# Second attention of a two-block kernel: scores of 64 rows in split precision, the bias added by the vector engine

## The reference

```python
q = rms_norm_2((h @ w_q).reshape(bsz, seqlen, N_HEADS, 2, HEAD_DIM), q_norm)
# k, v from shared_kv: k normed the same way, v has 128 columns a head
rel = k_pos[None, :] - q_pos[:, None]
bias = rel_bias[t5_causal_bucket(rel)].transpose(2, 0, 1)
s = jnp.einsum("bqhcd,bkhcd->bhcqk", qc, k) * HEAD_DIM ** -0.5
s = jnp.where(rel <= 0, s + bias[None, :, None], NEG_INF_2)
pm = jax.nn.softmax(s, axis=-1)
attn = pm[:, :, 0] - lam * pm[:, :, 1]
out = jnp.einsum("bhqk,bkhe->bqhe", attn, v)
```

## Time and profile before

| | |
|---|---|
| median of 3 runs | 2324.82 us |
| the profiled execution | 2324.46 us |
| its span | 2322.7 us |
| PE busy | 2128.9 us (92%) |
| DVE busy | 1281.0 us (55%) |
| ACT busy | 819.9 us (35%) |
| POOL busy | 466.5 us (20%) |
| mean granted clock of PE | 0.955 |

### The profile page before, as it was taken

How to read it: one execution, slowest core, us unless ns; L and a number is a source line. 1 busy time by engine, 2 the same in 40 slices (tenths; PEclk the granted TensorE clock), 3 DMA queues, 4 the chain that set the end, 5 groups by cost and what they waited for, 6 DMA issues and landing times.

```text
span 2322.7 us, 27094 instructions
## 1 busy us (share of the span) xinstructions
PE 2128.9 (92%) x9788; PEld 1681.1 (72%) x9788; DVE 1281.0 (55%) x1733; ACT 819.9 (35%) x1309; POOL 466.5 (20%) x596
## 2 busy tenths in 40 slices
PE   8999999999999454799999999999977899999999
PEld 8987668888887354687787877665655577877877
DVE  4253356464355698347747466633366467556455
ACT  3123333122235345534424234432144344334233
POOL 4052017970015784010000001100131000000000
PEclk9999989999999777899999999999899899999999
DMA  4220022232322100122222323221100122323222
GB/s 141 90 73 1 1 73 91 91 100 90 100 91 74 35 1 1 65 91 82 91 99 90 109 82 104 89 69 63 59 19 10 46 82 91 109 80 106 79 98 100
DMA packets 48592, 172.16 MB, mean 74 GB/s; under 512 B 5806, under 2 KB 6318, under 8 KB 48492
## 3 DMA queue, kind: packets, MB, share of 16 engines
q1 hardware_dynamic: 47164, 166.46, 21.6%
q0 software_dynamic: 1328, 4.37, 0.6%
HBM read 168.68 MB, written 2.12 MB: 74 GB/s over the span
## 4 chain that ended last, share of the span: by engine, by line
PE 84%; DVE 8%; ACT 5%; issue 2%; POOL 0%; DMA 0%; DVEq 0%; SPq 0%; ACTq 0%; POOLq 0%
PE ps L393 65%; PE ps L555 6%; PE ps L517 2%; ACT sq L1061 2%; PE ps L1390 1%; PE ps L499 1%; DVE t L1075 1%; PE ps L690 1%; ACT u_t L839 1%; PE ps L691 1%; PE ps L711 1%; PE ps L1392 1%; PE ps L1410 1%; ACT t L1458 1%; PE ps L1026 1%
## 5 line engine op out<-in xcount | busy, mean ns | idle before, releaser
L393 PE MATMUL ps<-x_hi,w_hi 128*128 128x512 f32 x1280 | 513.2, 401 | 5.0 <-DVE w_lo L379 4.9
L393 PE MATMUL ps<-x_lo,w_hi 128*128 128x512 f32 x1280 | 507.1, 396 | 0.0
L393 PE MATMUL ps<-x_hi,w_lo 128*128 128x512 f32 x1280 | 506.4, 396 | 0.0
L379 DVE TENSOR_TENSOR w_lo<-raw,w_hi 128x1024 fp32r<-128x1024 f32 x308 | 395.6, 1287 | 165.1 <-ACT w_hi L375 165.1
L375 ACT ACTIVATE w_hi<-raw 128x1024 fp32r<-128x1024 f32 x308 | 321.8, 1049 | 308.0 <-PE ps L393 136.6
L393 PE MATMUL ps<-a_hi,w_hi 128*128 128x512 f32 x928 | 372.0, 401 | 19.1 <-DVEq L360 11.2
L393 PE MATMUL ps<-a_hi,w_lo 128*128 128x512 f32 x928 | 369.6, 398 | 0.0
L393 PE MATMUL ps<-a_lo,w_hi 128*128 128x512 f32 x928 | 369.5, 398 | 0.0
L393 PEld LDWEIGHTS ps<-x_hi,w_hi 128*128 128x128 f32 x1280 | 241.1, 188 | 86.4 <-issue 22.2
L445 POOL TENSOR_TENSOR t<-t,sq 128x512 f32<-128x512 f32 x49 | 71.4, 1456 | 1116.0 <-ACT sq L436 1115.0
L393 PEld LDWEIGHTS ps<-x_lo,w_hi 128*128 128x128 f32 x1280 | 241.3, 189 | 56.8 <-issue 1.7
(11 more groups left out here) (322 smaller groups left out, 2704.7 us busy)
## 6 DMA issues: line engine op xcount, KB each, us to landing
raw<-in_wstream SPq DMA_DIRECT2D x308, 512.0 KB, 3.3
h<-in_xT SPq DMA_DIRECT2D x4, 528.0 KB, 7.3
b_raw<-scratch POOLq DMA_DIRECT2D x8, 256.0 KB, 3.5
out<-h SPq DMA_DIRECT2D x8, 256.0 KB, 2.0
p_raw<-in_pT POOLq DMA_DIRECT2D x2, 512.0 KB, 4.6
b_in_<-in_ssm_bc POOLq DMA_DIRECT2D x1, 512.0 KB, 4.3
c_raw<-in_ssm_bc POOLq DMA_DIRECT2D x1, 512.0 KB, 6.2
vecs<-in_vecs SPq DMA_DIRECT2D x1, 294.0 KB, 3.8
```

The costliest lines, as they stand in the source:

```text
L379: e.tensor_tensor(w_lo[:, u.slot, :], raw[:, u.c % 2, :], w_hi[:, u.slot, :], ALU.subtract)\
L393: last = e.matmul(ps[:, bank, :], wt[:, u.slot, w], x[:, k0 + k, 0:SEQ], start=(k == 0 and n == 0), stop=(k == kt - 1 and n == 2))
```

## The change

- The scores of a map are three fp32r products over that map's 64 rows (`q_hi` by `k_hi`, `q_hi` by `k_lo`, `q_lo` by `k_hi`). The scale is in q's norm gain (`gain_q`). `q_hi`, `k_hi` are written by ACT and `q_lo`, `k_lo` by POOL during the k and v projections; `k_hi` lies over `q2`, `k_lo` over `k2`. POOL's staging tiles go, `v` is turned from `v2` itself.
- The bias is added by DVE: `tensor_tensor_reduce` reads the scores from PSUM and the bias tile from SBUF, writes minus the sum into one of three SBUF tiles (`t0`, `t1`, `t2`) and gives the minimum. It takes the place of the maximum. The exponentials read from that tile in place. `b_hi`, `b_lo` and the flipped identity go.
- For this the bias rows must come in order: POOL writes each table row 128 times to DRAM, with a pitch of 641, and reads it back with a pitch of 640 (`bias_rows`, `bias_load`). Two bias tiles take turns.
- The order: PE does the scores of g, transposes of g-2, value products of g-3; DVE the maxima of g, then the mix of g-1; ACT copies the turned v after the exponentials; only the value products wait for it. The mix takes one reciprocal for both maps.
- The score slots are free when DVE's pass is done.

```diff
     with ExitStack() as c:
-        qs2 = sb("qs2", [P, 2, 2, SEQ], F32, c)
-        ks2 = sb("ks2", [P, 2, SEQ], F32, c)
-        vs2 = sb("vs2", [P, 2, SEQ], F32, c)
-        vtok = sb("vtok", [P, 2, 4, P], F32, c)
-        pt2 = sb("pt2", [P, 2, 4, P], F32, c)
-        b_hi = sb("b_hi", [P, 2, SEQ], F32R, c)
-        b_lo = sb("b_lo", [P, 2, SEQ], F32R, c)
+        q_hi = sb("q_hi", [P, 8, SEQ], F32R, c)
+        q_lo = sb("q_lo", [P, 8, SEQ], F32R, c)
     sb("region_a", [P, 2 * KT * SEQ])
...
+    with ExitStack() as c:
+        vtok = sb("vtok", [P, 2, 4, P], F32, c)
+        pt2 = sb("pt2", [P, 2, 4, P], F32, c)
+        bias1 = sb("bias1", [P, SEQ], F32, c)
     sb("region_x", [P, 2 * KT * TOK])
...
     with ExitStack() as c:
+        k_hi = sb("k_hi", [P, 8, SEQ], F32R, c)
+        k_lo = sb("k_lo", [P, 8, SEQ], F32R, c)
+    with ExitStack() as c:
         q2 = sb("q2", [P, 8, SEQ], F32, c)
...
-    scratch = nc.dram_tensor("scratch", (8, 640), F32, kind="Internal").ap()
+    scratch = nc.dram_tensor("scratch", (8, P * 641), F32, kind="Internal").ap()
...
+                if who == "act" and b > 1:
+                    qk_act(e, b, m - 1)
                 last(m - 1)
...
+    def qk_act(e, b, m):
+        e.wait_ge(hn_y, 8 * (b - 1) + m + 1)
+        if b == 3:
+            e.wait_ge(qk_lo, m + 1)
+        to, of = (q_hi, q2) if b == 2 else (k_hi, k2)
+        e.activation(to[:, m, :], of[:, m, :], ACT.Copy).then_inc(qk_hi, 1)
+
+    def qk_pool(e, b, m):
+        e.wait_ge(qk_hi, 8 * (b - 2) + m + 1)
+        e.wait_ge(hn_y, 8 * (b - 1) + m + 1)
+        hi, lo, of = (q_hi, q_lo, q2) if b == 2 else (k_hi, k_lo, k2)
+        e.tensor_tensor(lo[:, m, :], of[:, m, :], hi[:, m, :], ALU.subtract).then_inc(qk_lo, 1)
...
     def bias_load(e, p):
         if p >= 2:
-            e.wait_ge(s_mm, 32 + 4 * (p - 1))
...
+            e.wait_ge(nb_ok, 32 + 8 * (p - 1))
+        src = bass.AP(scratch.tensor, scratch.offset + p * P * 641 + P, [[640, P], [1, SEQ]])
+        e.dma_start((bias0, bias1)[p % 2][:, :], src).then_inc(b_in[p % 2], 16)
+
+    def bias_rows(e, p):
+        dst = bass.AP(scratch.tensor, scratch.offset + p * P * 641, [[P * 641, 1], [641, P], [1, 640]])
+        e.dma_start(dst, tab[p:p + 1, :].unsqueeze(1).to_broadcast([1, P, 640])).then_inc(tab_out, 16)
+
+    ST = (t0, t1, t2)
...
+        def pe_values(p):
+            ge(e, o_ok, p - 1)
+            for j in range(4):
+                last = e.transpose(ps[:, 6 + p % 2, j * P:(j + 1) * P], v2[:, p, j * P:(j + 1) * P], ident[:, :])
+            last.then_inc(vt_mm, 1)
+
         def pe_scores(g):
...
-            ge(e, exp_ok, 32 + 2 * (g - 1))
-            for c in range(2):
-                o = ps[:, 2 * sl + c, 0:N]
-                e.matmul(o, qs2[:, p % 2, c, qt * P:(qt + 1) * P], ks2[:, p % 2, 0:N], start=True, stop=False)
-                for n, t in enumerate((b_hi, b_lo)):
-                    last = e.matmul(o, flip_r[:, :], t[:, p % 2, SEQ - N:SEQ], start=False, stop=(n == 1))
+            if g >= 2:
+                e.wait_ge(nb_ok, 32 + 2 * (g - 1))
+            for n, (a, b) in enumerate(((q_hi, k_hi), (q_hi, k_lo), (q_lo, k_hi))):
+                for c in range(2):
+                    r = slice(HD * c, HD * c + HD)
+                    last = e.matmul(ps[:, 2 * sl + c, 0:N], a[r, p, qt * P:(qt + 1) * P], b[r, p, 0:N],
+                                    start=(n == 0), stop=(n == 2))
             last.then_inc(s_mm, 1)
...
         def pe_turn(g):
             e.wait_ge(nrm_ok, 32 + g + 1)
-            if qt == 0:
-                e.wait_ge(v2_ok, p + 1)
+            ge(e, pt_ok, 32 + g - 1)
...
         def pe_pv(g):
             if qt == 0:
-                ge(e, o_ok, p - 1)
+                e.wait_ge(v2_ok, p + 1)
...
         def dve_top(g):
             e.wait_ge(s_mm, 32 + g + 1)
+            if qt == 0:
+                e.wait_ge(b_in[p % 2], 16 * (p // 2 + 1))
+            if g >= 3:
+                e.wait_ge(pt_mm, 32 + g - 2)
             for c in range(2):
-                e.reduce_max(small[:, 1, 2 * sl + c:2 * sl + c + 1], ps[:, 2 * sl + c, 0:N], AX_X, negate=True)\
-                    .then_inc(nb_ok, 1)
...
+                e.tensor_tensor_reduce(ST[g % 3][:, c, 0:N], ps[:, 2 * sl + c, 0:N], (bias0, bias1)[p % 2][:, SEQ - N:SEQ],
+                                       -1.0, 3e38, ALU.add, ALU.min, small[:, 1, k + c:k + c + 1]).then_inc(nb_ok, 1)
...
         def dve_mix(g):
...
-            n = dve.did(e.reciprocal(r[0], small[:, 2, 2 * sl:2 * sl + 1]))
-            e.wait_ge(dve_did, n)
-            dve.did(e.tensor_scalar(t0[:, sl, 0:N], t0[:, sl, 0:N], r[0], None, ALU.mult))
-            e.wait_ge(exp_ok, 32 + 2 * g + 2)
-            n = dve.did(e.reciprocal(r[1], small[:, 2, 2 * sl + 1:2 * sl + 2]))
+            e.wait_ge(exp_ok, 32 + 2 * g + 2)
+            n = dve.did(e.reciprocal(small[:, 3, k:k + 2], small[:, 2, k:k + 2]))
             e.wait_ge(dve_did, n)
-            n = dve.did(e.tensor_tensor(r[1], r[1], neg_lam[:, :], ALU.mult))
+            n = dve.did(e.tensor_tensor(small[:, 3, k:k + 2], lam_pair[:, :], small[:, 3, k:k + 2], ALU.mult))
             e.wait_ge(dve_did, n)
+            n = dve.did(e.tensor_scalar(t[:, 0, 0:N], t[:, 0, 0:N], small[:, 3, k:k + 1], None, ALU.mult))
             e.wait_ge(dve_did, n)
...
         def act_exp(g):
...
+            for c in range(2):
+                e.wait_ge(nb_ok, 32 + 2 * g + c + 1)
+                e.activation(t[:, c, 0:N], t[:, c, 0:N], ACT.Exp, bias=small[:, 1, k + c:k + c + 1], scale=-1.0,
+                             accum_out=small[:, 2, k + c:k + c + 1]).then_inc(exp_ok, 1)
...
-        for g in range(32 + 2):
+        for g in range(32 + 3):
             if who == "pe":
                 if g < 32:
+                    if g % 4 == 0:
+                        pe_values(g // 4)
                     pe_scores(g)
-                if 1 <= g < 33:
-                    pe_turn(g - 1)
-                if g >= 2:
-                    pe_pv(g - 2)
+                if 2 <= g < 34:
+                    pe_turn(g - 2)
+                if g >= 3:
+                    pe_pv(g - 3)
             elif who == "dve":
+                if g < 32:
+                    dve_top(g)
                 if 1 <= g < 33:
                     dve_mix(g - 1)
-                if g == 0:
-                    dve_bias(0)
-                if g < 32:
-                    dve_top(g)
-                if g % 4 == 2 and g < 30:
-                    dve_bias(g // 4 + 1)
...
             else:
-                if g == 0:
-                    act_bias(0)
                 if g < 32:
                     act_exp(g)
+                    if g % 4 == 0:
+                        act_values(g // 4)
                 if 1 <= g < 33:
                     act_turn(g - 1)
-                if g % 4 == 1 and g < 29:
-                    act_bias(g // 4 + 1)
...
         e.wait_ge(tab_ok, 2)
-        e.dma_start(scratch, tab[0:8, :]).then_inc(tab_out, 16)
-        e.memset(qs2[:, :, :, :], 0.0).then_inc(qz2_ok, 1)
-        e.wait_ge(qz2_ok, 1)
-        e.wait_ge(tab_out, 16)
         for p in range(8):
+            bias_rows(e, p)
+        e.wait_ge(tab_out, 16 * 8)
+        bias_load(e, 0)
+        for b in (2, 3):
+            for m in range(KT):
+                qk_pool(e, b, m)
+        fence(e, 5)
+        for p in range(1, 8):
             bias_load(e, p)
-            if p == 0:
-                e.wait_ge(hn_y, 17)
-                e.wait_ge(unit_ev, U_KV + 9)
-            stage2_pool(e, p)
-            if p == 0:
-                fence(e, 5)
         fence(e, 6)
```

More of the change, by code:

```diff
@@ L175, in build @@
     gain_fs = sb("gain_fs", [P, KT])
-    neg_lam = sb("neg_lam", [P, 1])
+    lam_pair = sb("lam_pair", [P, 2])
+    gain_q = sb("gain_q", [P, 1])
     rel = sb("rel", [33, 8])
@@ L205, in build @@
         mask = sb("mask", [P, P], F32, c)
-        flip = sb("flip", [P, P], F32, c)
         wf_hi = sb("wf_hi", [P, KT, 8], F32R, c)
@@ L333, in build @@
     tab_out = sem("tab_out")
-    b_in = sem("b_in")
-    bhi_ok = sem("bhi_ok")
-    blo_ok = sem("blo_ok")
+    b_in = [sem(f"b_in{k}") for k in range(2)]
+    qk_hi = sem("qk_hi")
+    qk_lo = sem("qk_lo")
     lam_v = sem("lam_v")
@@ L1426, in act_bias @@
-        def act_bias(p):
-            e.wait_ge(b_in, 16 * (p + 1))
-            ge(e, s_mm, 32 + 4 * (p - 1))
-            e.activation(b_hi[:, p % 2, :], b_raw[:, 0, :], ACT.Copy).then_inc(bhi_ok, 1)
-        def dve_mix(g):
-            p, qt, sl = g // 4, g % 4, g % 2
-            N = (qt + 1) * P
-            r = [small[:, 3, 2 * sl + c:2 * sl + c + 1] for c in range(2)]
-            e.wait_ge(exp_ok, 32 + 2 * g + 1)
-            n = dve.did(e.reciprocal(r[0], small[:, 2, 2 * sl:2 * sl + 1]))
+                e.tensor_tensor_reduce(ST[g % 3][:, c, 0:N], ps[:, 2 * sl + c, 0:N], (bias0, bias1)[p % 2][:, SEQ - N:SEQ],
```

(26 more changed lines are left out.)

68 lines of the change are left out of this document (21 added, 47 removed).

## The result

The changed kernel takes 2342.19 us (median of 4 runs, 2339.78 to 2343.49) beside 2324.33 us for the kernel before. The ratio is 1.0072, with a 95% interval of 1.0057 to 1.0087. So it is slower, by 17.9 us, where 2288 us were forecast; the time lies outside the range of 2276 to 2326 as well.

A forecast was written before the change was run, and what follows sets the result against it. The second attention was taken as bound by a round trip PE, DVE, ACT, DVE, PE, afterwards by DVE; 2324.46 - 38 (stage) + 1 (later start) = 2287.5, forecast 2288 us, own range 2278 to 2299, wide range 2276 to 2326.

The forecast's parts named there:

- part 4: Work moved ahead of the second attention stage: row copies hidden up to 94 us, later opening of the stage costs 1.1 us.
- Price of the copies: Eight table row copies to DRAM: 11 us abreast on 16 engines, 127 to 174 us one after another.
- Rival 1: Row copies crowd the weight stream or come late: 7 to 32 us lost, 2295 to 2320 us; chance 0.26.
- Rival 2: Row copies in series take 174 us, PE waits for w_lo in the v projection: 2368 us; chance 0.13.
- Part 3: Second attention stage: DVE is the bound; with fill, drain and waits 95 us against 133, 38 us less.
- Part 1: Score products on PE: a 512-wide map costs 0.7 us, half of now; PE 67 us in the stage.
- The lower bound: Score products: the two maps, on different row halves, run side by side, half the cost again; -3 us in the range.
- The third rival: PE, busy for less time, clocks lower and bounds the stage; at 0.6 the stage is 110 us: 2303; chance 0.07.
- Part 2: DVE in the stage: new bias and minimum pass as long as the maximum, plus 6.4 us read-outs; 85 us (78 to 91).
- The fence: Start of the stage after the last scaling, copy and subtraction: opens at about 1672.4 us, cost 1.1 us.

The follow-up runs named there:

- e3: The changed kernel with the table put in DRAM first and the eight row copies reading it there, not from SBUF: 2285.04 us.
- e2: The kernel before with the eight row copies added, into a spare tensor nobody reads: 2382.67 us.
- e11: The changed kernel with a wait for each row copy ahead of the issue of the next: 2309.07 us.
- e13: e3 with both maps' score products taken from rows 0 to 63, the second map's own scores left out: 2293.00 us.
- e8: e3 with the copy of a finished head out of PSUM moved from DVE to ACT: 2275.24 us.
- e6: e3 with DVE's order turned back, the mix of g-1 ahead of the bias pass of g: 2297.84 us.
- e5: e3 with the three score passes of one map ahead of the other map's three: 2283.88 us.

## Why the prediction was wrong

The one step that failed is in part 4: "I take them as hidden: up to 94 us nothing is lost." It set the copies' time against one deadline only, that of POOL's q_lo at 1636 us. The copies met it nearly: they were in at 1637.3. What they missed is nobody's semaphore. They were on all 16 engines beside the weights, whose loads went from 3.2 to 46.3 us, and the weights have a lead of two tiles (raw, two buffers in turn), not 94 us. With the copies' source in DRAM (e3) the same kernel takes 2285.0 us, 3 from the forecast; below stands how much of that is luck. Point by point:

- *Price of the copies.* The bounds of 11 to 174 us hold 96. The Trainium skill's figure ("SBUF — State Buffer", "Door 1: The DMA port swizzle") gave 95, and that this is so near is in part luck. Part 4 has all copies read one partition, but each reads its own row of `tab`, eight partitions, which by that section are two ports and, abreast, 47 us, an estimate from it; they took 96 since they ran one behind the other. I gave the figure no weight in the sum since "no run here shows that", and I drew from it only a near miss of the slack. The port wasn't the missing piece; who else uses the engines was. (The 1024 packets of 2560 bytes are 512 of 5120 in the trace.)
- *Rival 1, copies that crowd the weights.* It is the true mechanism, and its price of 7 to 32 us was too low: e2 measures 58.6. "The weights held back for a unit or two" became 45 + 17 + 9 us of waits for them; a unit of PE is 5.75 us. Its "against", that the stream takes only a fifth of the engines' time, is true and says nothing: an engine whose packet waits for a slow source can't serve another, and 0.98 busy at 49 GB/s is what that looks like.
- *Rival 2, late q_lo, one for one past 94 us.* It didn't happen in the changed kernel. e11 makes it happen and confirms its deadline: 16 us late, 24 lost, of which 8 are the DVE split beside POOL.
- *Part 3, the stage.* 95 us forecast, 90.6 measured (91.5 in e3), so a gain of 42.3 for 38. The head period was to be 10.8 us; the chain has 1753.03 to 1763.62, 10.6.
- *Part 1.* The lower bound was the true one: 0.23 us for both maps (e3 beside e13), not 0.46. Scores are 1.9 us a head, not 3.8, at full clock. All the same PE is busy for 73.3 us of 90, more than the 67 forecast, at a clock of 0.79 and not 0.92:

```profile
1733.00:1823.00 90.00, 73.34 (x464) 57.31 (x462) 70.00 (x264) 55.49 (x169) 3.85 (x7) 0.79 0.07 21
```

  The clock explains only a part. 62 us less 15 for the scores, at 0.79, are 59; some of the other 14 is how the trace counts, with 0.40 us of busy time for a pair that is followed at 0.23, and the rest stays open. The third rival had the lower clock right, but not "busy for less of the time": PE was busy for 75% of the stage before and is for 81% now. Whether the clock cost anything in this stage no run shows.
- *Part 2.* DVE was to have 85 us of work and to be over 85% busy; it is busy for 70.0 us, 78%. The terms are right, read from the groups view of the stage:

```profile
L1431 DVE CUSTOM_DVE_ANT_0 t<-ps,bias 128x128 f32<-128x128 f32 (+3 forms) x64 | 28.7, 487 | 14.6 <-PE ps L1399 14.4
L1444 DVE SCALAR_TENSOR_TENSOR t<-t,small 128x128 f32<-128x128 f32 (+3 forms) x32 | 17.6, 552 | 1.1
...
L1442 DVE TENSOR_SCALAR t<-t,small 128x128 f32<-128x128 f32 (+3 forms) x32 | 12.4, 387 | 1.1
...
L1431 DVE DVE_READ_ACCUMULATOR2_ANT small<- 128x1 f32 x64 | 5.3, 83 | 0.0
```

  The pass takes 487 ns, the maximum took 485; the read-out is 83 ns. The Trainium skill's two instructions ("VectorE: DVE Perf Modes", "Two Vector instructions with no wait between them") are there, but their 5.3 us don't add. The sum of the groups is 79.7 us with reciprocals, products and copies (5.1 + 5.1 + 5.5), and the engine is busy 70.0, as instructions start before the last has ended:

```profile
1760.88 0.68 DVE L1431 CUSTOM_DVE_ANT_0 t<-ps,bias 128x512 f32<-128x512 f32 x1
1761.48 0.08 DVE L1431 DVE_READ_ACCUMULATOR2_ANT small<- 128x1 f32 x1
1761.48 0.69 DVE L1431 CUSTOM_DVE_ANT_0 t<-ps,bias 128x512 f32<-128x512 f32 x1
```

  A 0.68 us pass is followed by the next after 0.60. What I counted too much there was nearly made up by what I counted too little: 14.6 us of waits for scores, where I had 3. That the stage came within 5 us is in part this luck. DVE isn't the bound alone; PE and DVE wait for each other (PE 16.0 us for the mix), which fits e8, where more was gained than moved.
- *The fence.* +1.1 us forecast; from the last scaling's end to the first transposes it is 3.5 us for 1.9 before, 1.6 more. In e3 the last scaling itself ends at 1672.0 (1670.36 + 1.61), 2.6 us later than before, which I had at nothing. But 2.3 of it are there already where the table is copied out, ahead of the copies and the split:

```profile
1543.00 0.52 POOL L1595 DMA_DIRECT2D table<-tab  x1 [53.52 <-DVE tab L1867]
```

  Before, it is 1540.73, and e6, with the same work up to the stage, has it at 1538.48. So these 2.3 us are a difference of one execution to another and not a cost of the split.

The account of the profiled spans: the last scaling ends 59.8 us later (0.8 of it there at the table's copy, 57.2 gone in e3), the fence adds 1.6, the stage takes 42.3 off, and what follows it 1.5: 59.8 + 1.6 - 42.3 - 1.5 = 17.6, which is 2340.3 - 2322.7. (The forecast's own range doesn't follow from its bounds, which add to 2276 to 2298; nothing hangs on it.)

## What to carry to other kernels

Before a DMA is called hidden, price it by its source and ask who else uses the same engines while it is in the air; its own consumer's deadline is only one of the two. Here the broadcast from one SBUF partition was better read from DRAM; where it has to be slow, one in the air at a time let the weights through. And where the chain runs back and forth between two engines, a copy moved to a third can be worth more than its length: here 9.8 us for 4.8.

## What the runs showed of the hardware that I had not expected

- Eight DMAs of 320 KB that each read one of eight neighbouring SBUF partitions, 11.7 us apiece, raise the landing of 512 KB weight loads on another queue from 3.2 to 46.3 us, with all 16 engines 98% busy at 49 GB/s. With one of them in the air at a time it is 10.5 us, and ACT waits 0.6 us for weights in place of 70.9.
- The same bytes over the eight partitions in one DMA, on about half of the engines, take 55.6 us, and from DRAM about 16.
- Two fp32r passes of 64 rows on the two halves of the array cost 0.23 us together at 512 columns, on one half 0.47, and they start together even where the program has two other products between them (e5).
- A DVE subtraction of 128x1024 took 9.13 us in place of 1.24 beside eight POOL subtractions in a row.
